# A mixture-of-experts step on one core: the eighth gate chunk split like the others, and both output halves copied by ScalarE

## What is computed

```python
def hier_moe(h, w_rg, b_rg, w_re, b_re, w_gate, w_up, w_down):
    ...
    for g in range(N_EXPERT_GROUPS):
        cg = combine * (g_top == g).astype(jnp.float32)[:, None]
        a = jnp.einsum('td,edf->tef', hf, w_gate[g])
        b = jnp.einsum('td,edf->tef', hf, w_up[g])
        act = (jax.nn.silu(a) * b) * cg[..., None]
        y = y + jnp.einsum('tef,efd->td', act, w_down[g]).astype(jnp.float32)
    ...
```

## Time and profile before

| what | value |
|---|---|
| median of 3 runs | 960.84 us |
| the profiled execution | 961.21 us |
| its span | 959.4 us |
| PE busy | 928.8 us (97%) |
| VectorE busy | 690.0 us (72%) |
| ScalarE busy | 438.5 us (46%) |
| GpSimd busy | 93.9 us (10%) |
| granted TensorE clock, mean | 0.996 |

### The profile page before, as it was taken

One profiled execution on the slowest core, in us unless ns is written; L12 is line 12 of the kernel. 1 busy time (PEld: TensorE's weight loads), 2 busy tenths in 40 slices (PEclk: granted clock), 3 DMA queues, 4 the chain that ended last, 5 costly groups with the idle time before them and its releaser, 6 DMA issues.

```text
span 959.4 us, 13563 instructions
## 1 busy us (share of the span) xinstructions
PE 928.8 (97%) x5064; PEld 820.4 (86%) x5064; DVE 690.0 (72%) x935; ACT 438.5 (46%) x694; POOL 93.9 (10%) x109
## 2 busy tenths in 40 slices
PE   8999999999999999999999998999999999999984
PEld 6999999999999999999888887778787777777741
DVE  6548888778878845337621448899898988988947
ACT  7512221321121138722401324687878776777723
POOL 0000000010000000000000002322222122342100
PEclk9999999999999999999999999999999999999998
DMA  9020111111111210012511766589999999999558
GB/s 300 10 67 23 45 45 44 39 47 55 34 44 55 70 41 28 28 36 86 168 60 36 263 234 235 176 319 388 359 388 369 375 356 374 378 383 378 194 220 344
DMA packets 73803, 170.14 MB, mean 177 GB/s; under 512 B 10908, under 2 KB 48300, under 8 KB 60402
## 3 DMA queue, kind: packets, MB, share of 16 engines
q1 hardware_dynamic: 64529, 152.05, 44.4%
q0 software_dynamic: 9216, 17.32, 5.6%
HBM read 156.83 MB, written 22.47 MB: 187 GB/s over the span
## 4 chain that ended last, share of the span: by engine, by line
PE 82%; DMA 11%; DVE 4%; issue 1%; ACT 1%; SPq 1%; DVEq 0%; ACTq 0%; POOLq 0%
PE ps L1626 43%; PE ps L1915 11%; PE ps L1822 10%; DMA wgu<-in_w_up 8%; PE ps L1893 7%; DMA yy<-YK 2%; PE ps L1908 2%; PE ps L1871 2%; PE ps L1710 2%; PE ps L1776 1%; PE ps L1763 1%; PE ps L1649 1%; DMA xs<-in_x_prompt 1%; PE ps L1704 1%; PE ps L1879 1%
## 5 line engine op out<-in xcount | busy, mean ns | idle before, releaser
L1626 PE MATMUL ps<-hT,w_hi 128*128 128x352 f32 x1344 | 328.6, 326 | 0.1
L1626 PEld LDWEIGHTS ps<-hT,w_hi 128*128 128x128 f32 x1344 | 235.1, 188 | 1.1 <-DVE hT L1069 0.3
L1626 PE MATMUL ps<-hT,w_lo 128*128 128x352 f32 x672 | 218.1, 325 | 0.0
L1141 DVE SCALAR_TENSOR_TENSOR C<-V,w_dw,C 128x1086 f32<-128x1086 f32 x120 | 154.9, 1347 | 0.3
L1476 DVE TENSOR_TENSOR wgu_lo<-wgu,wgu_hi 128x1024 fp32r<-128x1024 f32 (+1 forms) x128 | 133.8, 1088 | 13.8 <-ACT wgu_hi L974 13.6
L974 ACT ACTIVATE wgu_hi<-wgu 128x1024 fp32r<-128x1024 f32 x124 | 113.5, 954 | 31.9 <-DMA wgu<-in_w_up 21.2
L1626 PEld LDWEIGHTS ps<-hT,w_lo 128*128 128x128 f32 x672 | 125.9, 187 | 0.0
L1915 PE MATMUL ps<-wgu_hi,XT_hi 128*128 128x512 f32 x224 | 99.6, 445 | 0.0
L1076 DVE TENSOR_TENSOR w_lo<-w_raw,w_hi 128x1024 fp32r<-128x1024 f32 (+1 forms) x44 | 45.3, 1029 | 66.3 <-ACT w_hi L778 66.3
L1822 PE MATMUL ps<-wo_hi,hT 128*128 128x512 f32 x288 | 91.7, 399 | 1.2 <-DVE wo_lo L1221 1.2
L1915 PE MATMUL ps<-wgu_hi,XT_lo 128*128 128x512 f32 x224 | 88.3, 394 | 0.0
(11 more groups left out here) (255 smaller groups left out, 1497.3 us busy)
## 6 DMA issues: line engine op xcount, KB each, us to landing
wgu<-in_w_gate SPq DMA_DIRECT2D x32, 1024.0 KB, 13.4
wgu<-in_w_up SPq DMA_DIRECT2D x32, 1024.0 KB, 16.9
wdn<-in_w_down SPq DMA_DIRECT2D x32, 1024.0 KB, 12.5
w_raw<-in_w_in SPq DMA_DIRECT2D x28, 512.0 KB, 3.9
yy<-YK SPq DMA_DIRECT2D x8, 1024.0 KB, 13.6
xs<-in_x_prompt SPq DMA_DIRECT2D x8, 512.0 KB, 7.6
wo_raw<-in_w_out SPq DMA_DIRECT2D x8, 512.0 KB, 4.5
xr<-in_x_prompt SPq DMA_DIRECT2D x16, 256.0 KB, 2.7
```

The source lines that it names most:

```text
L1141: op = dve.scalar_tensor_tensor(out=C[:, g, :], in0=V[:, g, k:k + CWID], scalar=w_dw[:, g, k:k + 1], in1=C[:, g, :], op0=ALU.mult, op1=ALU ...
L1626: op = pe.matmul(ps[:, bank_of(m, c), 0:CH], a[s][:, k, :], r[:, k, c * CH:(c + 1) * CH], start=(k == 0 and q == 0), stop=(k == K - 1 and ...
```

## The change

WHOLE becomes 0. All eight chunks of gate and up are then split, in four pieces of two chunks each: the last piece of ScalarE and VectorE grows from 128x512 to 128x1024, XT_hi and XT_lo grow from seven to eight chunks (128x728 to 128x832), PE does 24 split products per step and no plain one, and the tile XT with its copy and its memset is gone. ScalarE copies both halves of an expert's output, one after the other; VectorE only writes the scatter index, without a wait for the down product, and `down` waits for ScalarE alone. Of GpSimd's instructions none changes.

```diff
-WHOLE = 1
+WHOLE = 0
...
-        XT = at("XT", [P, WHOLE, P], F32, r_yp + 24576)
...
-        PREP = 10
+        PREP = 9
...
-                act.activation(XT[:, :, 0:CAP], ps[:, 0, :].rearrange("p (c t) -> p c t", c=4)[:, 0:WHOLE, 0:CAP], ACT.Copy)
                 act.activation(XT_hi[:, :, 0:CAP], split_chunks(), ACT.Copy).then_inc(s_xtA, 1)
...
-                act.activation(Y[u][0:CAP, 0:512], ps[0:CAP, 4 + 2 * (u % 2), :], ACT.Copy).then_inc(s_yA, 1)
+                for h in range(2):
+                    op = act.activation(Y[u][0:CAP, h * 512:(h + 1) * 512], ps[0:CAP, 4 + 2 * (u % 2) + h, :], ACT.Copy)
+                op.then_inc(s_yA, 1)
...
-            def y_out(it, u, uses, e):
-                dve.wait_ge(s_down, it + 1)
+            def s_column(u, uses, e):
                 wait(dve, s_ys[u], 16 * uses)
 
-                dve.tensor_copy(s_now[0:CAP, u:u + 1], column(s_idx, e))
-                dve.tensor_copy(Y[u][0:CAP, 512:1024], ps[0:CAP, 5 + 2 * (u % 2), :]).then_inc(s_yD, 1)
+                dve.tensor_copy(s_now[0:CAP, u:u + 1], column(s_idx, e)).then_inc(s_yD, 1)
...
-                for half in (XT[:], XT_hi[:].bitcast(F32), XT_lo[:].bitcast(F32)):
+                for half in (XT_hi[:].bitcast(F32), XT_lo[:].bitcast(F32)):
...
                 wait(pe, s_yA, it - 1)
-                wait(pe, s_yD, it - 1)
...
-                for c in range(WHOLE):
-                    pe.matmul(both, XT[:, c, :], wgu[u][:, :, c, :], start=(c == 0), stop=False)
                 pe.wait_ge(s_xtD, it + 1)
```

More of the change, by code:

```diff
@@ L1522, in step @@
                 if not (isinstance(i, int) and i == 0 and u == 0):
-                    y_out(it - 1, (u - 1) % WB, p * (GE // WB) + i + (u - 1) // WB, i * WB + u - 1)
+                    s_column((u - 1) % WB, p * (GE // WB) + i + (u - 1) // WB, i * WB + u - 1)
                 dve.wait_ge(s_athi, it + 1)
@@ L1573, in one @@
                 groups(dve, step, p)
-                y_out(p * GE + GE - 1, WB - 1, (p + 1) * (GE // WB) - 1, GE - 1)
+                s_column(WB - 1, (p + 1) * (GE // WB) - 1, GE - 1)
             rounds(dve, one)
```

## The result

The changed kernel takes **967.6 us** (median of 5 runs, 965.84 to 968.38) where the kernel before, timed beside it, takes 961.49 (959.77 to 962.47). The ratio is 1.0061 [1.0046, 1.0075]: slower by 6.1 us, where 2.7 was forecast. The direction was right, the size less than half of it. The profiled execution took 968.38 us, with a span of 966.6; that is 7.2 over the span of before and the upper end of the runs.

What follows compares the result with a forecast made beforehand. The DMA weight stream was taken to bound the expert stage. Start 1.4, last steps 0.35 and end 0.95 summed to +2.7 us: 963.9 us for the profiled execution, 963.5 on the median, range 959.2 to 966.8.

Steps and rivals of the forecast that it cites:

- Each microsecond that steps 0 and 1 lose on PE starts the gapless stream a microsecond later: Expert stage's start: the next down load waits for PE's first down product, so PE delays pass one to one to DMA.
- nothing in the middle: Middle expert steps: changes on PE, ScalarE and VectorE cost nothing, as DMA's 9.9 us a step covers PE's 9.5.
- PE's saving: Gate loop: 24 split matmuls take 5.59 us against 5.74, saving 0.15 us per step, counted as nothing in the middle.
- ScalarE's longer chain: Steady steps: second Y copy and longer XT_lo add about 0.6 us; as a rival wall, 969.1 us, chance 0.10.
- The rival of PE's pace: Middle steps: PE, not DMA, sets the pace, so 28 steps save 0.15 us each; 959.3 us, chance 0.16.
- the end's term: Last two output evictions: serial copies on ScalarE delay the last scatter and final norm; +0.95 us, bounds +0.5 and +1.1.
- The rival of a start that is taken up: After 626 us: gaps in the DMA stream absorb the late start, only the end counts; +1.3, 962.1 us, chance 0.22.
- One sign that the prediction set against itself: Middle steps: the prediction called itself wrong if PE waits for XT_lo there.
- the last steps' +0.35: Steps 29 to 31: PE waits for XT_lo, less its matmul saving; +0.35 us, between -0.45 and +0.8.
- the term of the start: Steps 0 and 1: PE waits for XT_lo, then has three more matmuls each, delaying the down load; +1.4 us.
- PE idles some 2 us, where it now idles 1.06: Step 0, before the gate loop: without the f32 pair PE waits longer for XT_lo, so its removal earns nothing there.
- the upper bound of 1.48: Steps 0 and 1: most the start could cost, 0.74 us per step from three more matmuls at 0.233 us.

Runs made afterwards that it cites:

- e6: Kernel before with 8 idle matmuls (3.6 us) on PE ahead of step 1's gate loop: +3.5 us, ratio 1.0033.
- e12: Kernel before with every down load in SP's loop placed behind the next expert's gate and up loads: 956.88 us, ratio 0.9953.
- e1: Changed kernel with the output copies of before, one half each by ScalarE and VectorE: +5.0 us on the kernel before, ratio 1.0057.
- e8: Changed kernel with 4 and 3 idle matmuls on PE during the XT_lo waits of steps 0 and 1: +3.05 us on the kernel before, ratio 1.0029.
- e4: Changed kernel, but ScalarE and VectorE share the output halves of the last two experts as before: +5.3 us on the kernel before, ratio 1.0055.
- e7: Kernel before with one extra 128 x 128 matmul (0.23 us) on PE in each of the middle loop's 20 steps: +0.4 us, ratio 1.0005.
- e10: Kernel before, down loads behind next gate and up except at loop turns, plus a 0.23 us matmul in 20 middle steps: −0.6 us, ratio 0.9994.
- e2: Kernel before, chunk 0 still plain f32, with both output halves copied by ScalarE: +1.0 us, ratio 1.0010.
- e3: Changed kernel with 8 and 6 idle matmuls on PE ahead of the gate loops of steps 0 and 1: +4.8 us on the kernel before, ratio 1.0042.

## Why the prediction was right and wrong

**Right: what sets the end.** "Each microsecond that steps 0 and 1 lose on PE starts the gapless stream a microsecond later" held: +3.48 at the load gave +3.5 in e6, and −3.78 gave −3.79 at the last scatter in e12. Down load and time moved together in e1 (+5.0 and +5.0), and in e8 (+1.8 and, with the end's 1.0, +3.05). That these agree so closely is in part luck: from the first down load to the last scatter the profiles of before, after, e1 to e4 and e6 to e8 take 293.2 to 295.0 us (the 0.76 of two copies at the end left out), so one profile shows the rule to about 1 us.

**Right: nothing in the middle.** PE's saving and ScalarE's longer chain both came to nothing in the time, and e7 and e10 show the cover (4.6 us of PE work for 0.4 and 0.1 us). The rival of PE's pace falls with them. The saving itself was smaller than the 0.15 us a step of the sum: over 18 steps from 636 us on the starts of x_turn are 9.43 us apart in the changed kernel (steps of 9.3 and 9.6 take turns), and 9.48 before, from 631. In e1, which leaves out the second copy on ScalarE, they are 9.30 apart, so ScalarE's longer chain takes back most of the saving, under the cover of DMA. As a wall it falls: e2, which holds its added copy, costs only the end's term. The rival of a start that is taken up falls with e6. One sign that the prediction set against itself came: PE waits for XT_lo in five steps from 811 to 873 us, 0.45 to 0.63 us each (the timeline shows none from 636 to 805). In that stretch steps of 10 us and more wait for weights; that the five waits cost nothing isn't shown by a run of their own, but e8's +3.05 leaves them little, with 1.8 at the load and 1.0 at the end.

**Right: the end.** Forecast +0.95, measured +1.0 in e2 (interval 0.1 to 1.9), of which 0.76 is seen between the Y copy and the scatter. With the last steps' +0.35 the forecast was 1.3; the rows put 7.50 − 5.75 = 1.75 behind the down load, and the 1.0 of it that is not the end's lies within the spread of the stream named above. So the term of the last steps is neither shown nor excluded; its sign, a wait for XT_lo in steps 29 and 30, is not in the changed kernel's trace.

**Wrong: the term of the start.** +1.4 was forecast and 5.0 measured. The step that failed is "PE idles some 2 us, where it now idles 1.06", right as a number (2.22) and then priced at its length alone. The idle time brought the clock down, 3.1 us over two steps, and the upper bound of 1.48 counted all matmuls at 0.233 us. No rival was about the clock, so the range's upper end, 966.8, missed it (its own terms add to 966.9). Of the 0.8 us by which 967.6 lies above, 0.65 is that the kernel before was timed at 961.49 beside it and not at 960.84; the miss of the term, 3.6 us, is none of that. A smaller part: "PE begins as before, near 608.3" left out the hand-over from VectorE. XT_lo ends at 608.02 + 1.03 = 609.05 and PE starts at 609.30, a delay of 0.25 us in each step, 0.5 us in all. With the clock held, e8 comes out at 963.99 us, against the 963.5 forecast: what the prediction did count came out within half a microsecond. One slip changes nothing: its rows give 0.83 ns a column of XT_hi, and not 0.84.

Still open: the clock fell in one of the two steps in e4's profile and in both in that of the changed kernel, so the loss differs from run to run (e4's six runs go from 962.94 us at a mean clock of 0.995 to 968.41 at 0.988), and what decides that was not tried.

## What to carry to other kernels

When a small operand is dropped from the front of a loop, ask what it covered: its matmuls may be what keeps PE from idling, and idle time is to be priced twice, as its length and as what the clock can take afterwards. Where a DMA stream sets the end, look at the instruction that starts the stream, since what delays it arrives at the end, and work elsewhere is free as long as the stream stays the slower of the two; in e12 it no longer was. An in-order queue of loads should follow the order in which buffers come free, at the loop's turn too: that was worth 5.0 us here (3.8 of them seen at the last scatter), and 0.7 with the old order left at the turn.

## What the hardware showed that was not expected

Idle gaps of 2.22 and 1.54 us in PE were followed by a clock at 1.2 GHz, with eight matmuls 0.43 us apart in each step. In the changed kernel the fall came about 1.5 us after work had begun again (609.30 to 610.8); in e1 the matmuls were slow at once, behind the same gap:

```profile
608.59 0.63 PE L1911 MATMUL ps<-wgu_hi,XT_hi 128*128 128x512 f32 x1 [2.21 <-DVE XT_lo L1481]
609.01 0.63 PE L1911 MATMUL ps<-wgu_hi,XT_lo 128*128 128x512 f32 x1
```

Not every gap does it. e4 has the same gap in step 0, and its clock was 1.00 from 608 to 616 us:

```profile
608.97 0.47 PE L1918 MATMUL ps<-wgu_hi,XT_hi 128*128 128x512 f32 x1 [2.21 <-DVE XT_lo L1483]
609.28 0.39 PE L1918 MATMUL ps<-wgu_hi,XT_lo 128*128 128x512 f32 x1
```

The trace of before has this row and a clock of 1.00 around it, from 588 to 600 us:

```profile
596.39 0.22 PE L1792 MATMUL ps<-A,tri_b 128*128 128x96 bf16 x1 [1.66 <-DVE A L1386]
```

In the changed kernel the clock was 0.72 over these 12 us, with the same code. There it was at its lower level from about 590.5 to 597 us, ahead of this row, and PE's longest wait from 585 to 591 us was 0.27 us; the idle matmuls then ran so long that the gap didn't come about. So a gap makes the fall likelier, as e3 and e8 show by filling it, but doesn't decide it, and a fall can come without one. The Trainium skill, "TensorE: Matmul & The Clock Gate", section "HAM oscillation — how this bites in real kernels", tells of a kernel in which waits between matmul groups brought the engine back to half rate each time. The trace here agrees on the rate, with 0.43 against 0.23 us a matmul, and differs on "each time": e4 had one fall in two steps.
